# Six row buffers in place of seven, ten weight chunks held over a layer's two token tiles in place of nine

## The reference, cut to what matters

```python
def hybrid_layer(x, ...):
    h = rmsnorm(x, g_mix)
    z = h @ w_in
    ...
    x = x + merged @ w_out
    x = x + peer_ffn(rmsnorm(x, g_ffn), w_peer_q, peer_keys, peer_u, peer_v)
    return x

def peer_ffn(x, w_q, sub_keys, u, v):
    ...
        q = (xc @ w_q).reshape(TOKEN_CHUNK, PEER_HEADS, 2, PEER_HALF)
        ...
        ug = u[eid]
        vg = v[eid]
        act = jax.nn.gelu(jnp.einsum('thkd,td->thk', ug, xc))
        y = jnp.einsum('thk,thkd->td', g * act, vg)
```

## Time and profile before

| | |
|---|---|
| time, median of 3 runs | 1605.27 us |
| lowest and highest run | 1602.56 and 1605.53 us |
| time of the profiled execution | 1605.11 us |
| its span, first to last instruction | 1603.3 us |
| mean granted TensorE clock | 0.958 |
| busy: PE, DVE, ACT, POOL | 84%, 68%, 58%, 42% |
| moved by DMA | 649.58 MB, mean 405 GB/s |

### The profile page before, as it was taken

How to read it: one execution, slowest core, us unless ns; L and a number is a source line. 1 busy time by engine, 2 the same in 40 slices (tenths; PEclk the granted TensorE clock), 3 DMA queues, 4 the chain that set the end, 5 groups by cost and what they waited for, 6 DMA issues and landing times.

```text
span 1603.3 us, 18944 instructions
## 1 busy us (share of the span) xinstructions
PE 1339.2 (84%) x5676; PEld 806.5 (50%) x5676; DVE 1096.5 (68%) x2608; ACT 931.9 (58%) x3344; POOL 668.7 (42%) x516
## 2 busy tenths in 40 slices
PE   8997878888987788877898878888988987778876
PEld 7984656644653356653465436655545532223222
DVE  1059978865777877745577887876667877777545
ACT  1216546567755745534775674555675666667766
POOL 0013434355444533424544353334453455455563
PEclk9999999999999998988999999999999999999999
DMA  7779999999999999999999999999999999999997
GB/s 294 291 300 423 422 424 422 423 422 412 388 422 417 415 420 423 422 424 424 420 410 423 418 409 425 422 423 422 375 422 422 421 394 420 422 421 422 415 421 292
DMA packets 91231, 649.58 MB, mean 405 GB/s; under 512 B 10056, under 2 KB 11512, under 8 KB 12536
## 3 DMA queue, kind: packets, MB, share of 16 engines
q0 software_dynamic: 73728, 536.90, 81.0%
q1 hardware_dynamic: 17076, 111.24, 17.0%
q10 hardware_dynamic: 324, 0.23, 0.1%
HBM read 647.28 MB, written 1.05 MB: 404 GB/s over the span
## 4 chain that ended last, share of the span: by engine, by line
DMA 53%; PE 20%; DVE 16%; ACT 5%; issue 5%; POOL 1%; DVEq 0%; ACTq 0%; POOLq 0%
DMA ring<-in_uv,expert 52%; PE ybank L612 10%; DVE ring L1041 7%; PE bank L423 5%; DVE xs L1054 3%; PE bank L561 2%; POOL ring L1172 1%; ACT wgt L787 1%; ACT diag L797 1%; ACT th L785 1%; DVE buf L876 1%; DVE picked L879 1%; ACT arg L782 1%; DMA wring<-in_chunks 1%; ACT sq L779 1%
## 5 line engine op out<-in xcount | busy, mean ns | idle before, releaser
L1172 POOL DMA_INDIRECT ring<-in_uv,expert x512 | 668.5, 1306 | 914.1 <-PE ybank L612 554.8
L612 PE MATMUL ybank<-ring,diag 128*128 128x512 f32 x1664 | 838.2, 638 | 239.7 <-ACT diag L797 234.6
L1041 DVE SCALAR_TENSOR_TENSOR ring<-ring,tok 128x1024 f32<-128x1024 f32 x512 | 625.9, 1224 | 384.3 <-DMA ring<-in_uv,expert 379.5
L612 PEld LDWEIGHTS ybank<-ring,diag 128*128 128x128 f32 x1664 | 303.2, 197 | 682.5 <-ACT diag L797 420.2
L779 ACT ACTIVATE sq<-dots 128x1 f32<-128x1 f32 x512 | 103.1, 201 | 525.5 <-DVE ring L1041 525.1
L423 PEld LDWEIGHTS bank<-hT,wring 128*128 128x128 f32 x2176 | 256.7, 196 | 23.0 <-issue 20.6
L423 PE MATMUL bank<-hT,wring 128*128 128x128 f32 x2176 | 259.0, 279 | 4.0 <-DVE hT L928 2.2
L787 ACT ACTIVATE wgt<-th,half_p 128x1 f32<-128x1 f32 x512 | 198.1, 387 | 17.1
L797 ACT ACTIVATE diag<-cst,wgt 128x128 f32<-128x128 f32 x416 | 167.0, 402 | 13.5
L785 ACT ACTIVATE th<-arg,dots 128x1 f32<-128x1 f32 x512 | 150.8, 295 | 16.6
L782 ACT ACTIVATE arg<-sq,gelu_bias 128x1 f32<-128x1 f32 x512 | 142.9, 279 | 0.0
(11 more groups left out here) (113 smaller groups left out, 735.3 us busy)
## 6 DMA issues: line engine op xcount, KB each, us to landing
wring<-in_chunks SPq DMA_DIRECT2D x84, 1024.0 KB, 9.2
held<-in_chunks SPq DMA_DIRECT2D x18, 1024.0 KB, 21.2
ring<-in_uv,expert POOLq DMA_INDIRECT x512, 12.1
xs<-in_x SPq DMA_DIRECT2D x2, 512.0 KB, 12.5
wpool<-in_w_pool SPq DMA_DIRECT2D x2, 512.0 KB, 13.7
trunk_out<-buf SPq DMA_DIRECT2D x4, 256.0 KB, 4.7
ring<-in_pool_scale SPq DMA_DIRECT2D x1, 512.0 KB, 8.4
cst<-in_consts SPq DMA_DIRECT2D x1, 448.0 KB, 6.0
```

Of the source, the lines that this page charges most:

```text
L612: ins = pe.matmul(ybank[m][:, :], diag[:, nth % DIAGS, :], ring[:, (2 * t + r) % RING, D + m * BANK:D + (m + 1) * BANK], start=(nth == ten ...
L1041: dve.scalar_tensor_tensor(out=ring[:, g % RING, 0:D], in0=ring[:, g % RING, 0:D], scalar=1.0, in1=tok[:, :], op0=ALU.mult, op1=ALU.mult, ...
L1172: pool.indirect_dma_start(ring[:, g % RING, :], None, uv, bass.IndirectOffsetOnAxis(ap=expert[:, at:at + 1], axis=0)).then_inc(row_landed[ ...
```

## The change

Two constants are changed. `held` gets a tenth chunk (chunk 25), which leaves the rotation, so that the rotation has 20 chunks; the ring of row buffers loses one. Both are 8 KB in each partition, so memory use stays as it was. No other line is touched; the loops, the waits and the assignment of rows to PE or DVE are computed from these constants or do not depend on them.

```diff
 W_SLOTS = 3
-HELD = 9
+HELD = 10
 HELD_CHUNKS = range(C_UP, C_UP + HELD)
 SLOT_CHUNKS = [c for c in range(CHUNKS) if c not in HELD_CHUNKS]
...
-RING = 7
+RING = 6
 TICKS = HK // 2
```

## The result

The change made the kernel slower: 1624.42 us in the median of four runs (1620.64 to 1631.62) against 1605.05 (1602.56 to 1605.53), a ratio of 1.0131 with a 95% interval of 1.0106 to 1.0155. Between the medians that is 19.4 us. The ratio is estimated from all the runs; by it the change costs 21.0 us, between 17.0 and 24.9.

What follows compares the result with a forecast made beforehand. After the start the kernel was taken as bound by bytes at 422 GB/s, with the seven-row ring just deep enough. 1605.11 - 4.97 (saved loads) + 19.9 (lost buffer) = 1620.0 us; range 1601.9 to 1640.

Steps and rivals of the forecast that it cites:

- The saving: At windows 1 and 3, one 1 MB chunk load fewer in each, where bytes bound the time: 4.97 us saved.
- The even stretch: Last long stretch before the end, 422 GB/s: six buffers suffice with 3.2 us to spare, so no cost.
- The buffer: In the thin DMA windows, one row buffer less lets the queue run dry longer: 19.9 us lost.
- eight dips: Eight of ten episodes of lowered DMA rate, each charged 2.49 us; the two shallowest charged nothing.
- the shortest flight: Gather issued at 411.68 with the queue empty: 6.35 us to its dot, used for a buffer's round trip.
- The sum: Whole kernel: 1605.11 less 4.97 plus 19.9 gives 1620.0 us, slower by 0.9%; chance 0.62.
- The signs named: Profile after: 512 ring loads, bytes down 2.1 MB, longer DVE gather waits, median flight toward 10 us, last stretch 422 GB/s.
- the same windows dip deeper: The windows already thin with seven buffers were to fall to 330 to 380 GB/s.
- The faster one: Thin windows get no deeper, added loss under 5 us, the 4.97 us kept: 1600.1 us; chance 0.11.
- That bytes and buffer cancel: Ten episodes cost about half a microsecond each, 5 us, cancelling the saving: 1605 us; chance 0.10.
- The much slower one: In thin windows the ring sets the pace, 240 us become 280: 1640.1 us; chance 0.17.

## Why the prediction was right

**The saving.** The term was 4.97 us for two loads at 422 GB/s. Measured alone in the other direction it is 6.3 us (4.0 to 8.7), and some 5.5 at six buffers. The term stands. One reading under it was generous: the pair of loads issued from 438.82 us begins in the eleventh slice (400.8 to 440.9 us), which moved 388 GB/s, and not wholly in the twelfth with its 422. What the rate that the Trainium skill gives for a core's HBM ("DMA: Bandwidth & Descriptors", section "Specifications", some 358 GB/s) would make of it, an estimate of 5.86 us, can't be told from it by these intervals; the rate itself can, as every kernel with six or more buffers has slices of 420 GB/s and more.

**The even stretch.** It was forecast to cost nothing with six buffers, and did (243.3 and 242.8 us). The time from issue to landing there has fallen as it had to. Before, the view of the tile ring for 1500 to 1580 us, then the changed kernel's for 1520 to 1600:

```profile
DMA to landing us min/median/max: 11.6/12.0/13.0
```

```profile
DMA to landing us min/median/max: 9.0/9.5/10.7
```

**The buffer.** The term was 19.9 us, eight dips at one row period. Measured alone it is 27.1 (24.4 to 29.9), and 24.6 (21.9 to 27.3) where seven buffers were made to act as six. This term was mis-sized by 5 to 7 us. The prediction put 2.49 us on each of eight dips, nothing on the rest, and set places that newly open against dips that cost less than a period. That balance did not hold. By the stretches above, with the bytes taken out, the six that had dips lost 25.6 us where the eight dips were to cost 19.9, among them 6.0 us where one dip was counted (rows 112 to 160) and 0.7 where one was counted too (rows 400 to 496); the two without a dip, rows 0 to 64 and 160 to 208, lost 7.6 where nothing was. These are the stretches of the slowest execution, 33.1 us in all. So the total fell within the range, but place by place the count is wrong, and that it came as near as it did owes something to luck.

A second step was wrong without showing in the sum: "the shortest flight", 6.35 us, was one lucky row. By it six buffers had 3.2 us to spare in an even stretch and five 0.7. The run with five buffers lacked 1.7 us (14.1 against 12.4). If six went round in 14.1 us as well, an estimate, their 14.9 us would leave 0.8 us to spare in the even stretch and not 3.2. The trace does not agree with the rule of the Trainium skill ("DMA: Bandwidth & Descriptors", section "Anatomy of one DMA — SWDGE (gpsimd) path") that a DMA on POOL's path takes some 2.0 us and its bytes over 436 GB/s, by estimate 4.4 us for 1 MB: the shortest landing in the changed kernel is 5.3 us, and the median, with other gathers ahead in the queue, 9.7.

**The sum.** 14.9 us were forecast and 21.0 measured by the ratio (17.0 to 24.9, the interval times 1605), 19.4 between the medians. The shortfall is the buffer's: 27.1 less 4.97 would be 22.1, within the measured interval. The median of 1624.42 us lies in the stated range of 1601.9 to 1640, which was wide enough for a buffer priced anywhere from 2 to 40 us.

**The signs named.** Bytes fell by 2.1 MB and the ring's loads stayed 512; DVE waits longer for gathers; the median flight fell to 9.7 us; the last even stretch stayed full. Wrong was that "the same windows dip deeper": by the clock some of them are full now, as the work has moved (800 to 820 us: 425 GB/s, where 401 were); only a comparison between the same rows shows the loss.

**The rivals.** The faster one needed a buffer worth less than 5 us; it is worth 27. That bytes and buffer cancel is out by the same number. The much slower one, 35 us, was too high for the change; with the pace going by the number of buffers in 240 us it would have given 40 us for the buffer alone, against 27.

## What to carry to other kernels

A ring of buffers ahead of a saturated queue has a knee: here the eighth buffer is worth about 3 us, if anything, the seventh 27, the sixth well over 100. Before trading depth for bytes, price both in a run of their own: a load saved in a byte-bound stretch is worth its bytes over the rate, and the depth can be tried without touching memory, by making the issuer wait for a later release. For a round trip don't take the shortest flight in the trace: here it was 6.35 us, and where a shallow ring set the pace the median was 7.4 to 8.6.

## What the runs showed that was not expected

The times of the changed kernel scatter. In its two sets of four runs it spread over 11.0 and 12.8 us, where the kernel before, run beside it, spread over 2.97 us in four runs and 5.8 us in seven. Its two profiled executions differ by 10 us, though the instructions are the same. One could think that a ring without spare time passes every small delay on; but six buffers with nine held chunks spread over 5.6 us and five buffers over 6.8, so this is not shown.

Eight buffers still show slices of 398 to 408 GB/s. Part of that is a queue that a late release empties; why the rate falls elsewhere with the engines busy is open.
